# Expert weights split in half units of 1024 columns instead of whole units of 2048

## The chip, the cores and the metric

The program runs on one core of a Trainium2 chip. The metric is the device time of one execution in microseconds (us), from the start of the program to its end; lower is better. The engines are called by the profile's names: PE is the matrix engine (PEld its loading of the stationary operand), DVE the vector engine, ACT the scalar engine, POOL GpSimd, SP the queue that issues most loads.

## What is computed

Two streams (256 new frames, and 64 frames that continue a running stream, 320 tokens in all) pass two layers. A layer mixes tokens (a short convolution and a gated linear attention behind one input projection, then an output projection), adds and normalizes, and then mixes channels: dense in layer 0, experts in layer 1. The part that the change touches is the experts:

```python
def _swiglu(x, w_gate, w_up, w_down):
    return (jax.nn.silu(x @ w_gate) * (x @ w_up)) @ w_down

def _moe(x, router, w_gate, w_up, w_down):
    ...
    top_v, top_i = lax.top_k(logits, TOP_K)
    gates = jax.nn.softmax(top_v, axis=-1)
    ...
    for e in range(N_EXPERTS):
        y = y + combine[:, e:e + 1] * _swiglu(xf, w_gate[e], w_up[e], w_down[e])
```

There are 8 experts, each with three matrices of 1024 x 3584 in float32. All results are float32, and a token goes to its 2 best experts.

## The kernel before

**Split products.** A float32 product is made of three faster ones in a rounded format (fp32r). Each weight w is split into whi, which is w rounded, and wlo = w - whi; each input likewise. PE adds whi times the high input, wlo times the high input and whi times the low input. ACT makes whi by a copy that rounds (`round_unit`, L988 to L993), DVE makes wlo by a subtraction (`rest_unit`, L1247 to L1250).

**Units and rings.** Weights come in units of 1 MiB, 128 partitions x 2048 columns. SP loads them in the order of their use into `raw`, a ring of RAW = 6 units (`load`, L387 to L391); ACT and DVE write whi and wlo into rings of SPLIT = 3 units. There are 410 units: 74 for both mixers and the dense layer, and from U_MOE = 74 on 336 for the experts. Four kinds of semaphore tie a unit's way together, and each counts one per unit: `raw_landed` (a load is in), `hi_ready` (ACT is done), `lo_ready` (DVE is done; PE may start the unit, and SP may load unit n + 6 over it) and `unit_used` (PE is done; ACT may write unit n + 3 over it).

**The order of the work on experts** is written out by hand in `pair_steps`, and every engine walks the same list of steps: four pairs of experts, in each 14 chunks of 512 hidden columns (seven for one expert, seven for the other). A chunk c has two gate units, two up units and two down units; the down units are those of chunk c - 1, and one step "T" (PE transposes the hidden values, four transposes, L931) stands between the gate units. A gate or up unit is 12 matmuls (four k-tiles x three products, L901 to L903), a down unit 12 matmuls as well (two k-tiles x three products x two halves of the output, L918). A group below means these six units with their T. At the end of each pair but the last come four gather steps "X" (L877), in which PE picks the next pair's token rows. The last pair has a different end and one extra transposing step, "GT" (L936, chunk 6).

**Where the split stands in the order.** At unit n, ACT and DVE first issue the split of unit n + 2 (AHEAD = 2), and then what belongs to n:

```python
                        if not last or unit + AHEAD <= PER_PAIR:
                            rest_unit(n + AHEAD, i, PER_PAIR)
                        if part == "up" and half:
                            dve.wait_ge(unit_used, upto(n + 1, i, PER_PAIR))
                            dve.wait_ge(m_silu, upto(c + 1, i, PC))
                            dve.tensor_tensor(hm[:, c % 2, :], ...).then_inc(m_hid, 1)
```

So DVE's product `hm` (L1738), which waits until PE is through with the second up unit n, stands behind the split of n + 2 and ahead of that of n + 3. Behind `hm`, still ahead of the split of n + 3, DVE has further work in some chunks: small tables of the router in chunks 0 to 7 of the first pair (`tables`), the rows of tokens in chunks 0 to 4 of the last pair (`rows_of_tokens`), the weighted sum of finished experts in chunks 6 to 11 of the last pair (`combine`, L1723, after a gather from memory that POOL issues, L565) and `acc_lo` in chunks 11 to 13 (L1756). ACT has Silu (L1191) behind the second gate unit, the rounding of the transposed hidden values (`hT_hi`, L1215) at T, `acc_hi` (L1197) in chunks 11 to 13 of the last pair, and in chunk 13 of the last pair a load of another function table (L1193).

## Time and profile before

| what | value |
|---|---|
| median of 3 runs | 1661.7 us (1661.43 to 1662.46) |
| the profiled execution | 1663.22 us |
| its span, first to last instruction | 1661.6 us |
| PE busy | 1630.2 us, 98% of the span |
| DVE busy | 1228.0 us, 74% |
| ACT busy | 982.5 us, 59% |
| from the router's end to the last expert matmul | about 639 to 1643 us of the span |

Busy is the share of time in which at least one instruction of the engine ran. PE's matmuls overlap in the records, so a PE that is busy all the time may still have lost something: what counts for PE is the distance from one matmul's start to the next. The table is an average; the experts' stretch alone is what the change touches.

### The profile page before, as it was taken

To read this page: it belongs to the slowest core of one execution; us is meant where nothing else is said; L and a number is where in the kernel's file an instruction comes from. 1 tells how busy PE (TensorE), PEld (TensorE's weight loads), DVE (VectorE), ACT (ScalarE), POOL (GpSimd) and SP (SyncE) were. 2 spreads that over 40 slices of the span, in tenths; PEclk is the share of its full clock that TensorE was granted. 3 is DMA by queue.
4 is the path that set the end of the run, shared out by engine and by line. 5 is a ranking of instruction groups with operands and counts; after the bars stand their busy time and mean duration, and the time that the engine had idled before them with its cause. 6 is when DMAs were issued, how large, how long until landed. Compare 5 with 4: busy or idle time off the path is not lost.

```text
span 1661.6 us, 22901 instructions
## 1 busy us (share of the span) xinstructions
PE 1630.2 (98%) x8756; PEld 1413.9 (85%) x8756; DVE 1228.0 (74%) x1050; ACT 982.5 (59%) x820; POOL 82.9 (5%) x91
## 2 busy tenths in 40 slices
PE   8999999999999999999999999999999999999996
PEld 7999999999989998787888888888888888777775
DVE  4567545445454766989887888887888888989987
ACT  4453433333344536777776777776777776776663
POOL 1001111111010000000000000000000000120200
PEclk8999999999999999999999999999999999999999
DMA  9424444444444243999998999998999999999992
GB/s 297 133 97 134 152 151 146 145 145 146 150 153 153 77 134 132 354 365 362 373 376 314 363 371 364 378 363 321 369 375 368 365 364 349 354 382 377 372 352 77
DMA packets 226500, 446.58 MB, mean 269 GB/s; under 512 B 10514, under 2 KB 72640, under 8 KB 226368
## 3 DMA queue, kind: packets, MB, share of 16 engines
q1 hardware_dynamic: 223856, 434.13, 73.5%
q0 software_dynamic: 2560, 11.29, 1.8%
q8 instruction: 58, 0.95, 0.2%
q14 instruction: 26, 0.21, 0.0%
HBM read 439.87 MB, written 8.67 MB: 270 GB/s over the span
## 4 chain that ended last, share of the span: by engine, by line
PE 88%; DVE 6%; ACT 2%; issue 2%; DMA 1%; SPq 1%; DVEq 0%; ACTq 0%
PE ps L918 15%; PE ps L901 12%; PE ps L903 12%; PE ps L902 12%; PE ps L590 10%; PE ps L592 10%; PE ps L591 10%; DVE wlo L1250 2%; ACT whi L993 2%; PE ps L877 1%; PE ps L931 1%; DMA raw<-in_moe_w_up 1%; PE ps L663 1%; PE ps L622 1%; DVE xl L1285 1%
## 5 line engine op out<-in xcount | busy, mean ns | idle before, releaser
L1250 DVE TENSOR_TENSOR wlo<-raw,whi 128x2048 fp32r<-128x2048 f32 x410 | 934.5, 2291 | 255.3 <-ACT whi L993 252.6
L993 ACT ACTIVATE whi<-raw 128x2048 fp32r<-128x2048 f32 x410 | 784.5, 1915 | 244.5 <-PE ps L592 85.1
L901 PE MATMUL ps<-whi,xg 128*128 128x512 f32 x896 | 360.9, 403 | 10.5 <-DVE wlo L1250 10.2
L903 PE MATMUL ps<-whi,xg 128*128 128x512 f32 x896 | 355.1, 396 | 0.0
L902 PE MATMUL ps<-wlo,xg 128*128 128x512 f32 x896 | 354.8, 396 | 0.0
L590 PE MATMUL ps<-xh,whi 128*128 128x320 f32 x832 | 259.8, 312 | 0.3
L591 PE MATMUL ps<-xl,whi 128*128 128x320 f32 x832 | 256.9, 309 | 0.0
L592 PE MATMUL ps<-xh,wlo 128*128 128x320 f32 x832 | 256.8, 309 | 0.0
L901 PEld LDWEIGHTS ps<-whi,xg 128*128 128x128 f32 x896 | 169.3, 189 | 55.4 <-DVE wlo L1250 15.5
L903 PEld LDWEIGHTS ps<-whi,xg 128*128 128x128 f32 x896 | 169.2, 189 | 40.1
L902 PEld LDWEIGHTS ps<-wlo,xg 128*128 128x128 f32 x896 | 169.4, 189 | 36.9
L590 PEld LDWEIGHTS ps<-xh,whi 128*128 128x128 f32 x832 | 156.5, 188 | 5.2 <-DVE xl L1285 2.4
L591 PEld LDWEIGHTS ps<-xl,whi 128*128 128x128 f32 x832 | 156.5, 188 | 0.2
L592 PEld LDWEIGHTS ps<-xh,wlo 128*128 128x128 f32 x832 | 156.4, 188 | 0.0
L918 PE MATMUL ps<-whi,hT_hi 128*128 128x512 f32 x448 | 140.8, 395 | 1.3 <-DVE wlo L1250 0.7
L918 PE MATMUL ps<-whi,hT_lo 128*128 128x512 f32 x448 | 141.0, 396 | 0.0
L918 PE MATMUL ps<-wlo,hT_hi 128*128 128x512 f32 x448 | 140.5, 394 | 0.0
L918 PEld LDWEIGHTS ps<-whi,hT_hi 128*128 128x128 f32 x448 | 83.9, 188 | 21.8 <-DVE wlo L1250 2.1
L918 PEld LDWEIGHTS ps<-whi,hT_lo 128*128 128x128 f32 x448 | 84.3, 188 | 19.9
L918 PEld LDWEIGHTS ps<-wlo,hT_hi 128*128 128x128 f32 x448 | 84.2, 188 | 19.9
L1215 ACT ACTIVATE hT_hi<-ps 128x512 fp32r<-128x512 f32 x56 | 33.6, 600 | 75.1 <-PE ps L931 74.8
L590 PE MATMUL ps<-hh,whi 128*128 128x320 f32 x224 | 69.0, 308 | 0.0
(287 smaller groups left out, 1378.8 us busy)
## 6 DMA issues: line engine op xcount, KB each, us to landing
raw<-in_moe_w_gate SPq DMA_DIRECT2D x112, 1024.0 KB, 7.4
raw<-in_moe_w_up SPq DMA_DIRECT2D x112, 1024.0 KB, 7.4
raw<-in_moe_w_down SPq DMA_DIRECT2D x112, 1024.0 KB, 6.9
raw<-in_w_in SPq DMA_DIRECT2D x24, 1024.0 KB, 5.5
raw<-in_ffn_w_gate SPq DMA_DIRECT2D x14, 1024.0 KB, 5.0
raw<-in_ffn_w_up SPq DMA_DIRECT2D x14, 1024.0 KB, 5.0
raw<-in_ffn_w_down SPq DMA_DIRECT2D x14, 1024.0 KB, 5.0
raw<-in_w_out SPq DMA_DIRECT2D x8, 1024.0 KB, 5.2
```

The source lines that it names most:

```text
L590: pe.matmul(out, wh, hi, start=start and j == 0, stop=False)
L591: pe.matmul(out, wh, lo, start=False, stop=False)
L592: mm = pe.matmul(out, wl, hi, start=False, stop=stop and j == len(pairs) - 1)
L622: pe.matmul(bank[:, 0:P], mean_d[:], mean_d[:], start=True, stop=True)
L663: pe.matmul(ps[5][:, 0:T], mean_d[:], sq[:, k % 4, :], start=k == 0, stop=k == KT - 1).then_inc(var_part, 1)
L901: pe.matmul(bank[:], xh_k, wh, start=k == 0, stop=False)
L902: pe.matmul(bank[:], xh_k, wl, start=False, stop=False)
L903: mm = pe.matmul(bank[:], xl_k, wh, start=False, stop=k == KT - 1)
L918: mm = pe.matmul(ps[4 + d][:], hT[:, c % 2, k, :], slot(w, n, SPLIT, 2)[:, j, 512 * d:512 * d + 512], start=fc == 0 and k == 0 and hT is h ...
L993: act.activation(flat(whi, n, SPLIT), flat(raw, n, RAW), ACT.Copy).then_inc(hi_ready, 1)
L1215: act.activation(hT_hi[:, c % 2, :, :].rearrange("p f s -> p (f s)"), bank[:], ACT.Copy).then_inc(hT_hi_ready, 1)
L1250: dve.tensor_tensor(flat(wlo, n, SPLIT), flat(raw, n, RAW), flat(whi, n, SPLIT).bitcast(F32), ALU.subtract).then_inc(lo_ready, 1)
```

## The change

The experts' units (n >= U_MOE) are rounded, subtracted and waited for in two halves of 1024 columns. The rings keep their three and six whole units. All three semaphores now count in half units: for the other 74 units ACT, DVE and PE add 2 at once, and every wait's number is doubled. For an expert unit ACT runs two copies of 1024 columns, each with its own wait on `unit_used` and an increment of `hi_ready`; DVE runs two subtractions of 1024 columns, each with its own wait on `hi_ready` and an increment of `lo_ready`; PE waits before the unit's first and before its seventh matmul, and increments `unit_used` after its sixth and twelfth. The first half of a gate or up unit is its first two k-tiles, that of a down unit its first k-tile, which are the first six matmuls. The load of a whole unit still waits for both halves of the one that it overwrites. Silu, `hm`, the copies of finished experts and all steps' order stay.

```diff
+        def part(t, n, ring, h):
+            return flat(t, n, ring)[:, UNIT // 2 * h:UNIT // 2 * h + UNIT // 2]
+
...
                 if n >= RAW:
-                    sp.wait_ge(lo_ready, upto(n - RAW + 1, i, per))
+                    sp.wait_ge(lo_ready, upto(2 * (n - RAW + 1), i, 2 * per))
                 sp.dma_start(slot(raw, n, RAW, a), src).then_inc(raw_landed[n % RAW], 16)
...
                         bank = ps[2 * (c % 2) + (part == "up")]
-                        pe.wait_ge(lo_ready, upto(n + 1, i, PER_PAIR))
                         for j in range(4):
                             k = 4 * half + j
+                            if j % 2 == 0:
+                                pe.wait_ge(lo_ready, upto(2 * n + j // 2 + 1, i, 2 * PER_PAIR))
...
                             mm = pe.matmul(bank[:], xl_k, wh, start=False, stop=k == KT - 1)
-                        mm.then_inc(unit_used, 1)
+                            if j % 2:
+                                mm.then_inc(unit_used, 1)
...
-                        pe.wait_ge(lo_ready, upto(n + 1, i, PER_PAIR))
                         for j in range(2):
                             k = 2 * half + j
+                            pe.wait_ge(lo_ready, upto(2 * n + j + 1, i, 2 * PER_PAIR))
...
-                        mm.then_inc(unit_used, 1)
+                            mm.then_inc(unit_used, 1)
...
                 act.wait_ge(raw_landed[n % RAW], upto(16 * (n // RAW + 1), i, 16 * (per // RAW)))
-                if n >= SPLIT:
-                    act.wait_ge(unit_used, upto(n - SPLIT + 1, i, per))
-                act.activation(flat(whi, n, SPLIT), flat(raw, n, RAW), ACT.Copy).then_inc(hi_ready, 1)
+                if n < U_MOE:
+                    if n >= SPLIT:
+                        act.wait_ge(unit_used, upto(2 * (n - SPLIT + 1), i, 2 * per))
+                    act.activation(flat(whi, n, SPLIT), flat(raw, n, RAW), ACT.Copy).then_inc(hi_ready, 2)
+                    return
+                for h in range(2):
+                    act.wait_ge(unit_used, upto(2 * (n - SPLIT) + h + 1, i, 2 * per))
+                    act.activation(part(whi, n, SPLIT, h), part(raw, n, RAW, h), ACT.Copy).then_inc(hi_ready, 1)
...
-                dve.wait_ge(hi_ready, upto(n + 1, i, per))
-                dve.tensor_tensor(flat(wlo, n, SPLIT), flat(raw, n, RAW), flat(whi, n, SPLIT).bitcast(F32),
-                                  ALU.subtract).then_inc(lo_ready, 1)
+                if n < U_MOE:
+                    dve.wait_ge(hi_ready, upto(2 * (n + 1), i, 2 * per))
+                    dve.tensor_tensor(flat(wlo, n, SPLIT), flat(raw, n, RAW), flat(whi, n, SPLIT).bitcast(F32),
+                                      ALU.subtract).then_inc(lo_ready, 2)
+                    return
+                for h in range(2):
+                    dve.wait_ge(hi_ready, upto(2 * n + h + 1, i, 2 * per))
+                    dve.tensor_tensor(part(wlo, n, SPLIT, h), part(raw, n, RAW, h), part(whi, n, SPLIT, h).bitcast(F32),
+                                      ALU.subtract).then_inc(lo_ready, 1)
...
                         if part == "up" and half:
-                            dve.wait_ge(unit_used, upto(n + 1, i, PER_PAIR))
+                            dve.wait_ge(unit_used, upto(2 * (n + 1), i, 2 * PER_PAIR))
```

The waits on `unit_used` and `lo_ready` in the mixers and the dense layer are doubled in the same way and not shown.

What this does to the order is seen at two places. The first is DVE in the last pair, chunk 6: the split of unit n + 2, then `hm`, then two sums into `acc`, then the splits of n + 3, n + 4 and n + 5 (REGISTER_ALU computes the number of a wait). Before:

```order
L1249 REGISTER_ALU
L1250 TENSOR_TENSOR wlo<-raw,whi 128x2048 [waits hi_ready]
L1737 REGISTER_ALU [waits unit_used]
L1738 TENSOR_TENSOR hm<-sg,ps 128x512 [waits m_silu]
L1723 SCALAR_TENSOR_TENSOR acc<-y,gate_at,acc 128x1024 [waits y_fetched0]
L1723 SCALAR_TENSOR_TENSOR acc<-y,gate_at,acc 128x1024 [waits combined,y_fetched1]
L1249 REGISTER_ALU
L1250 TENSOR_TENSOR wlo<-raw,whi 128x2048 [waits hi_ready]
```

And in the changed kernel:

```order
L1267 TENSOR_TENSOR wlo<-raw,whi 128x1024 [waits hi_ready]
L1266 REGISTER_ALU
L1267 TENSOR_TENSOR wlo<-raw,whi 128x1024 [waits hi_ready]
L1754 REGISTER_ALU [waits unit_used]
L1755 TENSOR_TENSOR hm<-sg,ps 128x512 [waits m_silu]
L1740 SCALAR_TENSOR_TENSOR acc<-y,gate_at,acc 128x1024 [waits y_fetched0]
L1740 SCALAR_TENSOR_TENSOR acc<-y,gate_at,acc 128x1024 [waits combined,y_fetched1]
L1266 REGISTER_ALU
L1267 TENSOR_TENSOR wlo<-raw,whi 128x1024 [waits hi_ready]
```

Nothing changes its place; each subtraction has become two, with a wait of its own. The second place is PE, the gate or up unit in the last pair behind GT. Before, one wait per twelve matmuls:

```order
L901 MATMUL ps<-whi,xg 128x512 [waits lo_ready]
L902 MATMUL ps<-wlo,xg 128x512
L903 MATMUL ps<-whi,xg 128x512
L901 MATMUL ps<-whi,xg 128x512
L902 MATMUL ps<-wlo,xg 128x512
L903 MATMUL ps<-whi,xg 128x512
L901 MATMUL ps<-whi,xg 128x512
L902 MATMUL ps<-wlo,xg 128x512
```

In the changed kernel one wait per six:

```order
L906 MATMUL ps<-whi,xg 128x512 [waits lo_ready]
L907 MATMUL ps<-wlo,xg 128x512
L908 MATMUL ps<-whi,xg 128x512
L906 MATMUL ps<-whi,xg 128x512
L907 MATMUL ps<-wlo,xg 128x512
L908 MATMUL ps<-whi,xg 128x512
L903 REGISTER_ALU
L906 MATMUL ps<-whi,xg 128x512 [waits lo_ready]
L907 MATMUL ps<-wlo,xg 128x512
```

The matmuls are the same ones in the same order, and the seventh now waits as well.

## Rows read from the trace of the kernel before

**Rows 1.** The page: busy time of each engine, and the rate of loads in 40 slices.

```profile
PE 1630.2 (98%) x8756; PEld 1413.9 (85%) x8756; DVE 1228.0 (74%) x1050; ACT 982.5 (59%) x820; POOL 82.9 (5%) x91
...
GB/s 297 133 97 134 152 151 146 145 145 146 150 153 153 77 134 132 354 365 362 373 376 314 363 371 364 378 363 321 369 375 368 365 364 349 354 382 377 372 352 77
```

**Rows 2.** The page's costliest groups: count, busy us, mean ns, idle before, releaser.

```profile
L1250 DVE TENSOR_TENSOR wlo<-raw,whi 128x2048 fp32r<-128x2048 f32 x410 | 934.5, 2291 | 255.3 <-ACT whi L993 252.6
...
L901 PE MATMUL ps<-whi,xg 128*128 128x512 f32 x896 | 360.9, 403 | 10.5 <-DVE wlo L1250 10.2
```

**Rows 3.** Timeline, 1000 to 1012 us, second pair: start, duration, engine, line, operation.

```profile
1001.59 0.63 PE L918 MATMUL ps<-whi,hT_hi 128*128 128x512 f32 x2
...
1001.79 1.92 ACT L993 ACTIVATE whi<-raw 128x2048 fp32r<-128x2048 f32 x1 [0.88 <-PE ps L903]
...
1003.75 2.29 DVE L1250 TENSOR_TENSOR wlo<-raw,whi 128x2048 fp32r<-128x2048 f32 x1
...
1007.19 0.40 PE L901 MATMUL ps<-whi,xg 128*128 128x512 f32 x1
```

**Rows 4.** Timeline of ACT: the rounding of the transposed hidden values, once per group.

```profile
657.36 0.60 ACT L1215 ACTIVATE hT_hi<-ps 128x512 fp32r<-128x512 f32 x1 [1.24 <-PE ps L931]
...
796.91 0.60 ACT L1215 ACTIVATE hT_hi<-ps 128x512 fp32r<-128x512 f32 x1 [1.25 <-PE ps L931]
...
1189.82 0.60 ACT L1215 ACTIVATE hT_hi<-ps 128x512 fp32r<-128x512 f32 x1 [1.31 <-PE ps L931]
1206.98 0.60 ACT L1215 ACTIVATE hT_hi<-ps 128x512 fp32r<-128x512 f32 x1 [1.31 <-PE ps L931]
...
1402.93 0.60 ACT L1215 ACTIVATE hT_hi<-ps 128x512 fp32r<-128x512 f32 x1 [1.32 <-PE ps L931]
...
1621.21 0.60 ACT L1215 ACTIVATE hT_hi<-ps 128x512 fp32r<-128x512 f32 x1 [1.47 <-PE ps L931]
```

**Rows 5.** Timeline, last pair, chunk 6: DVE, then PE in a narrower window.

```profile
1501.32 0.68 DVE L1738 TENSOR_TENSOR hm<-sg,ps 128x512 f32<-128x512 f32 x1
1501.91 2.67 DVE L1723 SCALAR_TENSOR_TENSOR acc<-y,gate_at,acc 128x1024 f32<-128x1024 f32 x2
1504.50 6.69 DVE L1250 TENSOR_TENSOR wlo<-raw,whi 128x2048 fp32r<-128x2048 f32 x3
...
1506.84 0.50 PE L901 MATMUL ps<-whi,xg 128*128 128x512 f32 x1 [1.32 <-DVE wlo L1250]
1507.18 0.39 PE L902 MATMUL ps<-wlo,xg 128*128 128x512 f32 x1
```

**Rows 6.** Timeline, last pair, chunk 11: operations of 1024 columns on ACT and DVE.

```profile
1590.00 1.04 ACT L1197 ACTIVATE acc_hi<-acc 128x1024 fp32r<-128x1024 f32 x1
...
1595.32 1.21 DVE L1756 TENSOR_TENSOR acc_lo<-acc,acc_hi 128x1024 fp32r<-128x1024 f32 x1
1596.46 6.68 DVE L1250 TENSOR_TENSOR wlo<-raw,whi 128x2048 fp32r<-128x2048 f32 x3
```

**Rows 7.** Timeline, 625 to 650 us, the first expert unit that is split behind the router.

```profile
642.43 3.70 ACT L993 ACTIVATE whi<-raw 128x2048 fp32r<-128x2048 f32 x2
...
644.37 6.70 DVE L1250 TENSOR_TENSOR wlo<-raw,whi 128x2048 fp32r<-128x2048 f32 x3 [4.21 <-ACT whi L993]
...
646.72 0.50 PE L901 MATMUL ps<-whi,xg 128*128 128x512 f32 x1 [2.33 <-DVE wlo L1250]
```

**Rows 8.** Windows: length, busy us (x count) of PE, PEld, DVE, ACT, POOL; PEclk, DMA, GB/s.

```profile
647.70:651.00 3.30, 3.30 (x9) 2.55 (x9) 3.30 (x2) 0.71 (x1) 0.00 (x0) 0.50 1.02 309
...
1500.00:1600.00 100.00, 93.71 (x409) 74.52 (x408) 90.88 (x54) 69.97 (x46) 10.46 (x4) 1.00 1.01 374
```

**Rows 9.** Timeline of PE, last pair, chunk 13: two late starts.

```profile
1630.29 0.73 PE L918 MATMUL ps<-whi,hT_hi 128*128 128x512 f32 x2 [0.74 <-DVE wlo L1250]
...
1637.11 0.73 PE L918 MATMUL ps<-whi,hT_hi 128*128 128x512 f32 x2 [0.54 <-DVE hT_lo L1764]
```

**Rows 10.** The chain of waits, 1380 to 1500 us: the longest piece (start, us, what).

```profile
1456.41 15.37 DMA raw<-in_moe_w_up
```

More of the change, by code:

```diff
@@ L604, in two_tiles @@
                         if j == KT - 1:
-                            mm.then_inc(unit_used if half else tile_done, 1)
+                            mm.then_inc(unit_used, 2) if half else mm.then_inc(tile_done, 1)
             def x_hi(k):
@@ L756, in mixer @@
                 hooks = {1: gates, 5: turn_kv, 6: scores, 7: states, 8: outputs, 9: mean_squares}
-                pe.wait_ge(lo_ready, U_IN[l] + 1)
+                pe.wait_ge(lo_ready, 2 * (U_IN[l] + 1))
                 two_tiles(U_IN[l], lambda j: pe.wait_ge(xl_ready, KT * 2 * l + j + 1))
@@ L769, in mixer @@
                     n = U_IN[l] + u
-                    pe.wait_ge(lo_ready, n + 1)
+                    pe.wait_ge(lo_ready, 2 * (n + 1))
                     for half in range(2):
@@ L774, in mixer @@
                         mm = split_product(ps[(2 * u + half) % 4][:, 0:T], by_tile(n, KT, half), True, True)
-                        mm.then_inc(unit_used if half else tile_done, 1)
+                        mm.then_inc(unit_used, 2) if half else mm.then_inc(tile_done, 1)
                     if u in hooks:
@@ L780, in mixer @@
                     n = U_OUT[l] + u
-                    pe.wait_ge(lo_ready, n + 1)
+                    pe.wait_ge(lo_ready, 2 * (n + 1))
                     if u == 0:
@@ L789, in mixer @@
                         mm = split_product(ps[m % 4][:, 0:T], by_tile(n, KT, half, y_hi, y_lo), True, True)
-                        mm.then_inc(unit_used if half else tile_done, 1)
+                        mm.then_inc(unit_used, 2) if half else mm.then_inc(tile_done, 1)
                 pe.wait_ge(rows_ready[l], 1)
@@ L800, in dense_mixer @@
                         n, q = U_FFN + j, j // 2
-                        pe.wait_ge(lo_ready, upto(n + 1, c, PER_CHUNK))
+                        pe.wait_ge(lo_ready, upto(2 * (n + 1), c, 2 * PER_CHUNK))
                         if j == 0:
@@ L812, in dense_mixer @@
                             mm = split_product(ps[bank][:, 0:T], by_tile(n, KT, half), True, True)
-                            mm.then_inc(unit_used if half else tile_done, 1)
+                            mm.then_inc(unit_used, 2) if half else mm.then_inc(tile_done, 1)
                     n = U_FFN + 4
-                    pe.wait_ge(lo_ready, upto(n + 1, c, PER_CHUNK))
+                    pe.wait_ge(lo_ready, upto(2 * (n + 1), c, 2 * PER_CHUNK))
                     pe.wait_ge(d_added, upto(4, c, 8))
@@ L822, in dense_mixer @@
                             mm = split_product(ps[4 + m][:, 0:T], [(wh, wl, hh[:, k, :], hl[:, k, :])], k == 0, k == 3)
-                    mm.then_inc(unit_used, 1)
+                    mm.then_inc(unit_used, 2)
                     n = U_FFN + 5
-                    pe.wait_ge(lo_ready, upto(n + 1, c, PER_CHUNK))
+                    pe.wait_ge(lo_ready, upto(2 * (n + 1), c, 2 * PER_CHUNK))
                     for m in range(4):
@@ L830, in dense_mixer @@
                                  for k in range(4)]
-                        split_product(ps[m][:, 0:T], pairs, True, True).then_inc(unit_used if m == 3 else tile_done, 1)
+                        mm = split_product(ps[m][:, 0:T], pairs, True, True)
+                        mm.then_inc(unit_used, 2) if m == 3 else mm.then_inc(tile_done, 1)
                 pe.wait_ge(d_added, 8 * FC + 4)
@@ L921, in pair @@
                                                        stop=fc == FC - 1 and k == 3 and hT is hT_lo)
-                        mm.then_inc(unit_used, 1)
+                            mm.then_inc(unit_used, 1)
                     else:
@@ L1110, in mixer @@
                         if half:
-                            act.wait_ge(unit_used, n + 1)
+                            act.wait_ge(unit_used, 2 * (n + 1))
                         else:
@@ L1137, in dense_mixer @@
                                 if half:
-                                    act.wait_ge(unit_used, upto(U_FFN + j + 1, c, PER_CHUNK))
+                                    act.wait_ge(unit_used, upto(2 * (U_FFN + j + 1), c, 2 * PER_CHUNK))
                                 else:
@@ L1188, in pair @@
                         if part == "gate" and half:
-                            act.wait_ge(unit_used, upto(n + 1, i, PER_PAIR))
+                            act.wait_ge(unit_used, upto(2 * (n + 1), i, 2 * PER_PAIR))
                             act.wait_ge(m_hid, upto(max(0, c - 1) + 1, i, PC))
@@ L1199, in pair @@
                             a = c // FC
-                            act.wait_ge(unit_used, upto(n + 1, i, PER_PAIR))
+                            act.wait_ge(unit_used, upto(2 * (n + 1), i, 2 * PER_PAIR))
                             if last and a:
@@ L1480, in mixer @@
                         if half:
-                            dve.wait_ge(unit_used, n + 1)
+                            dve.wait_ge(unit_used, 2 * (n + 1))
                         else:
@@ L1506, in dense_mixer @@
                                 if half:
-                                    dve.wait_ge(unit_used, upto(n + 1, c, PER_CHUNK))
+                                    dve.wait_ge(unit_used, upto(2 * (n + 1), c, 2 * PER_CHUNK))
                                 else:
@@ L1518, in dense_mixer @@
                                 if j == 4 or m == 3:
-                                    dve.wait_ge(unit_used, upto(n + 1, c, PER_CHUNK))
+                                    dve.wait_ge(unit_used, upto(2 * (n + 1), c, 2 * PER_CHUNK))
                                 else:
@@ L1532, in clear @@
             def clear():
-                dve.wait_ge(unit_used, U_OUT[1] + UNITS_OUT)
+                dve.wait_ge(unit_used, 2 * (U_OUT[1] + UNITS_OUT))
                 dve.memset(xt_hi[TOK[2]:P, 2, :].bitcast(F32), 0.0)
```

## The prediction

> **What bounds the kernel now.** I read the page first. PE is busy for 98% of the span, DVE for 74%, ACT for 59% [rows 1]; so PE sets the time, and a change on DVE and ACT can only pay where PE waits for them. The page's groups name such waits: before L901, PE's idle time is ended by DVE's wlo, 10.2 us in all [rows 2]. That figure is too low, because a matmul is recorded with 0.39 us [rows 5] while the next one starts after 0.23 (2.79 us for the twelve of a unit, below): 0.16 is missing from each idle time. I therefore measured the loss by distances between starts.
>
> The timeline of the second pair shows the undisturbed rhythm [rows 3]. From PE's start on a unit at 1001.59 to its start two units later at 1007.19 are 5.60 us, so 2.80 us a unit (2.79 in the third pair, whose groups are 6 x 0.01 shorter). When PE starts unit n (1001.59), ACT gets the slot that unit n - 1 has left 0.20 us later, rounds n + 2 in 1.92, DVE subtracts in 2.29 until 1006.04, and PE needs the result at 1007.19. The way through the ring takes 4.45 us of 5.60, and 1.15 are spare: PE is the bound there. In the third pair a whole group of six units with its T takes 1206.98 - 1189.82 = 17.16 us [rows 4]; the same distance in the other two stretches shows the loss. In the first pair, 657.36 to 796.91 are 8 groups in 139.55 us, 2.3 over 8 x 17.16. In the last, 1402.93 to 1621.21 are 12 groups in 218.28, 12.4 over 12 x 17.16, of which I give 0.6 to the GT step (three transposes, by the four of a T: a group of 17.16 less six units of 2.79 is 0.42), so 11.8.
>
> Why PE waits there is seen in chunk 6 of the last pair [rows 5]. DVE's hm waits for PE's second up unit n, but it stands behind the split of n + 2, which through the ring ends 4.45 us after PE began n, that is 1.65 after PE has finished it. Only then come hm (0.59 to the next start), the extra work E, and the split of n + 3, which PE wants 5.58 us after the end of n. This leaves for E 5.58 - 1.57 - 0.59 - 2.29 - 0.06 = 1.07 us (1.57 since DVE starts the next operation 0.08 before the record of the last ends; 0.06 is from DVE's end to PE's start). E here is 1504.50 - 1501.91 = 2.59, so PE should be 1.5 late; its row at 1506.84 shows 1.32 idle beside the overlap. The tables and sums of the other chunks are the same case with another E.
>
> **The change, part by part.**
> 1. *Cost on DVE.* 336 subtractions of 2048 become 672 of 1024. Back to back, the three at 1504.50 give (6.69 - 2.29)/2 = 2.20 us apart [rows 5]; an operation of 1024 with two inputs takes 1.21, and the next starts 1.14 after it [rows 6]. So a unit costs 2.28 instead of 2.20: 0.08, or 27 us more over 336 units. Beside PE, DVE then needs 12 x 1.14 + 2 x 0.60 = 14.9 us of 17.16 in a group, so it is covered; in a group with E = 2.59 it is 17.5, 0.3 over, once in each of three groups, which the spare time gained below takes up.
> 2. *Cost on ACT.* A rounding of 1024 takes 1.04 [rows 6] and one of 2048 takes 1.92 [rows 3]: at most 0.16 more a unit, 54 us in all, on an engine with 679 us idle. Covered by PE.
> 3. *Cost on PE.* 336 more waits, one before each seventh matmul. Between units PE already has such a wait, satisfied ahead of time, and the group of 17.16 contains six of them at 2.79 a unit; twelve starts at the usual 0.23 are the same 2.79. Lower bound 0. The upper bound is a wait that really holds: the restart at 1506.84 has 0.34 to the next start instead of 0.23 [rows 5], so 0.11 each, 37 us in all. I take 0, since the nearest row is a satisfied wait. Loads, POOL and SP's queue keep their number and order; SP's wait is met earlier, never later.
> 4. *Gain inside the ring.* ACT may round the first half of n + 2 when PE is half through n - 1, at -1.40 + 0.20 = -1.20 counted from PE's start of n, and is done at -0.16; DVE has the first half at +1.09. The second half starts on ACT at +0.20 and is through DVE at 0.20 + 1.04 + 0.04 + 1.21 = +2.49, instead of +4.45. That is before PE ends n at 2.80, so hm no longer stands behind it. Then 0.20 + 0.59 + E + 1.21 + 0.06 must fit into 5.58: E up to 3.52 instead of 1.07. The 2.59 of chunks 6 to 8 fits. In chunk 11 the two sums and acc_lo come to about 2.59 + 1.14 = 3.7, just over the edge, so 0.2 stay there. What is late next is nothing of this chain, so I count the whole of both stretches, less that: 2.3 + 11.6.
> 5. *Gain at the start.* Behind the router, ACT comes to unit 2 of the experts only at 642.43, its copy of it begins there, and PE, which could go on at 644.2 (2.33 of idle time and the missing 0.16 back from there), starts at 646.72 [rows 7]. In halves: 642.43 + 1.04 + 0.04 + 1.21 + 0.06 = 644.8, so the wait of 2.5 shrinks to 0.6, 1.9 gained. Just behind that wait the granted clock is 0.50 for 3.3 us, half of what 2.4 GHz is, and PE starts 9 matmuls where it would start 14 [rows 8], 1.65 us lost. The window with the waits of 1.5 us in chunks 6 to 8 has a mean granted clock of 1.00 [rows 8], so behind a wait of 0.6 I expect no such stretch: 1.65 gained. Together 3.6.
> 6. *Gain at the end.* In chunk 13 PE starts late twice, by 0.74 and 0.54 of idle time, with the missing 0.16 by 0.9 and 0.7 [rows 9]: the first behind ACT's table load, the second behind DVE's order. Both chains are shortened by over 1 us; 1.6 gained.
> 7. *Not gained.* Chunks 4 and 5 of the last pair waited for a load that took 15.37 us [rows 10], while POOL's gathers used the same engines. A late load now leads to PE 1.04 + 1.21 + 0.1 = 2.4 after it lands instead of 4.3, which helps, but PE no longer gives the loads time by waiting elsewhere. I keep back 1.0.
>
> Sum: 2.3 + 11.6 + 3.6 + 1.6 - 1.0 = 18.1 us less. From the profiled execution's 1663.2 this is 1645.1; the median of the runs stands 1.5 below that execution, so 1643.6.
>
> **A rule against it.** In rows 5 three held subtractions follow each other 2.20 apart though each is recorded with 2.29. The Trainium skill, VectorE: DVE Perf Modes, The DRAIN you can't avoid, says that the next operation doesn't start until the pipe is empty, and its rules for authors say to minimize the number of operations. By that rule the halves would cost more than in part 1, and the sum would be that of the first rival below; the rows don't bear it out for this form.
>
> **The rivals.**
> - *Each half pays in full.* If no half overlaps its neighbour and each waits 0.04 for its semaphore, a half costs 1.25, a group 12 x 1.25 + 2 x 0.72 = 16.4. Quiet groups stay hidden. Groups with E = 2.59 need 19.0 and run 1.9 over, less the 2 us of spare time once: about 3.5 us of their 4.7 stay. The same in chunk 11 (2 us) and the first pair (1) leaves 12 of 18.1: about 1650. For it: the new halves wait on ACT's halves one by one. Against: rows 5 and 6.
> - *Loads become the bound.* A unit is 1.049 MB; at the highest rate of any slice, 382 GB/s [rows 1], it takes 2.74 us, and PE wants one in 17.16/6 = 2.86. The reserve is 4%. After the delay of [rows 10] the loads would catch up by only 0.12 a unit, so in chunks 4 to 8 the waits would move from DVE to the loads. Of 6 us there 4 stay: 1647. Against: the load isn't asked for later than before.
> - *The seventh matmul's wait costs PE time* (slower). It decides from 18.1/336 = 0.054 us a wait. At the 0.11 of a real restart [rows 5] it is 37 us, so 19 slower: 1680. For it: the wait is in the middle of an accumulation, where the trace of before has none. Against: satisfied waits between units show nothing.
> - *No change*: the first halves would have to reach PE no earlier, as when ACT, in order, is held by the second half's wait ahead of Silu or hT_hi, and these come late for PE in turn. ACT's 41% of idle time speaks against it; 1661.
>
> **How the numbers follow.** Forecast 0.64, first rival 0.14, loads 0.12, slower 0.06, no change 0.04. The predicted time is the forecast's, 1643.6. Its own bounds are 1640.5 (the 1.0 kept back, the 0.2 of chunk 11 and the 0.6 of the start gained as well, and 1.3 for some 20 groups of the second pair's kind, 0.07 longer than the third pair's, that might run like these) and 1647; reaching to the loads and the first rival gives 1640.5 to 1650.5, which leaves out the last two and the tails. A measurement can tell 0.2% (3.3 us) from no change: faster 0.90, same 0.04, slower 0.06.
>
> **What would show it.** Groups in both stretches near 17.2 us; hm right behind PE's second up unit instead of behind wlo; subtractions of about 1.21 us, starting 1.14 apart when back to back; no low clock behind the router's end; PE's unit at 2.79 with no gap at its seventh matmul. I would be wrong if that gap shows, if groups with sums stay near 18.8, or if ACT's idle time is ended by loads for many units.

## The result, and the profile after

| what | before | changed |
|---|---|---|
| median, six runs each | 1661.72 us (1660.17 to 1662.46) | 1649.24 us (1648.18 to 1653.08) |
| ratio, 95% interval | | 0.9929, 0.9916 to 0.9942 |
| profiled execution, its span | 1663.22, 1661.6 us | 1648.18, 1646.5 us |
| PE, DVE, ACT busy | 1630.2, 1228.0, 982.5 us | 1621.7, 1244.0, 1015.9 us |

The change is 12.5 us faster by the medians, 0.71%. 1643.6 had been forecast, with a range of 1640.5 to 1650.5. So the sign and the range held, and a third of the gain of 18.1 is missing. The two profiled executions stand 15.1 us apart in their spans: the one of before lay 1.5 above its median, the one of the change 1.1 below. Where the steps are compared below, it is against these 15.1. A unit has the number of its place in its pair, from 0 to 83; chunk c begins at unit 6c. A quiet group is one in which PE waits for nothing.

First the costliest groups of the page, changed kernel, as in [rows 2]:

```profile
L1267 DVE TENSOR_TENSOR wlo<-raw,whi 128x1024 fp32r<-128x1024 f32 x672 | 778.2, 1219 | 54.2 <-ACT whi L1004 53.0
L1004 ACT ACTIVATE whi<-raw 128x1024 fp32r<-128x1024 f32 x672 | 676.7, 1054 | 94.1 <-PE ps L924 55.1
L906 PE MATMUL ps<-whi,xg 128*128 128x512 f32 x896 | 358.8, 400 | 2.8 <-DVE wlo L1267 2.6
```

There are 672 halves on either engine, of 1.22 and 1.05 us each, and PE's idle time ended by wlo has gone from 10.2 to 2.6 us. The change's DVE is busy for 16 us more, ACT for 33. Next ACT's timeline at the lines that answer to [rows 4]:

```profile
653.41 0.60 ACT L1226 ACTIVATE hT_hi<-ps 128x512 fp32r<-128x512 f32 x1 [1.61 <-PE ps L937]
790.74 0.60 ACT L1226 ACTIVATE hT_hi<-ps 128x512 fp32r<-128x512 f32 x1 [2.17 <-PE ps L937]
...
1124.24 0.60 ACT L1226 ACTIVATE hT_hi<-ps 128x512 fp32r<-128x512 f32 x1
...
1150.47 0.60 ACT L1226 ACTIVATE hT_hi<-ps 128x512 fp32r<-128x512 f32 x1 [1.54 <-PE ps L937]
1167.64 0.60 ACT L1226 ACTIVATE hT_hi<-ps 128x512 fp32r<-128x512 f32 x1 [2.17 <-PE ps L937]
...
1397.81 0.60 ACT L1226 ACTIVATE hT_hi<-ps 128x512 fp32r<-128x512 f32 x1 [2.18 <-PE ps L937]
...
1606.73 0.60 ACT L1226 ACTIVATE hT_hi<-ps 128x512 fp32r<-128x512 f32 x1 [2.18 <-PE ps L937]
```

The eight groups of the first stretch take 137.33 us, 17.17 each: no loss is left there. The twelve groups of the last stretch take 208.92 instead of 218.28; 12 x 17.16 + 0.6 would be 206.5, so 2.4 are left. A place that the prediction didn't look at has become longer: from 1124.24, in the last chunk of the second pair, to 1150.47 in the first of the third are 26.23 us, where before it was 23.90. Sorted by stretches, the 15.1 us are: start 3.95 (from 657.36 to 653.41), first stretch 2.22, last stretch 9.36, end 0.62, quiet groups of the middle pairs 1.3, and -2.33 at the border of the second and third pair.

Of the 3.95, 0.69 are there before PE starts the first expert unit (638.64 before, 637.95 after).

**Start.** Timelines of ACT, DVE and PE behind the router, changed kernel, as in [rows 7]:

```profile
641.75 3.89 ACT L1004 ACTIVATE whi<-raw 128x1024 fp32r<-128x1024 f32 x4
...
642.83 8.04 DVE L1267 TENSOR_TENSOR wlo<-raw,whi 128x1024 fp32r<-128x1024 f32 x7 [3.35 <-ACT whi L1004]
...
644.11 0.50 PE L906 MATMUL ps<-whi,xg 128*128 128x512 f32 x1 [0.41 <-DVE wlo L1267]
```

ACT begins at 641.75, the first half has gone through DVE 2.3 us later, and PE stands idle for 0.41 instead of 2.33. No stretch of granted clock 0.50 follows: the trace records none from here until PE has finished at 1636.7.

**Sums of the last pair.** DVE's timeline, chunk 6, changed kernel, as in [rows 5]:

```profile
1489.89 4.68 DVE L1267 TENSOR_TENSOR wlo<-raw,whi 128x1024 fp32r<-128x1024 f32 x4
1494.48 0.68 DVE L1755 TENSOR_TENSOR hm<-sg,ps 128x512 f32<-128x512 f32 x1
1495.08 2.67 DVE L1740 SCALAR_TENSOR_TENSOR acc<-y,gate_at,acc 128x1024 f32<-128x1024 f32 x2
1497.66 4.62 DVE L1267 TENSOR_TENSOR wlo<-raw,whi 128x1024 fp32r<-128x1024 f32 x4
```

The same E of 2.58 now leads from 1497.66 to a first half at 1498.88 and to PE's start at 1498.93, 0.3 late instead of 1.5. The split of n + 2 still stands ahead of hm as four halves back to back, ending 4.68 us after 1489.89; what has changed is that behind the sums PE waits for one half instead of a whole.

**The new stop.** Timelines of ACT, then PE, where the loop over the middle pairs jumps back (changed kernel):

```profile
1133.75 1.09 ACT L1219 ACTIVATE ys<-ps 128x512 f32<-128x512 f32 x2 [1.27 <-PE ps L924]
1138.87 3.90 ACT L1004 ACTIVATE whi<-raw 128x1024 fp32r<-128x1024 f32 x4 [4.03 <-PE ps L908]
...
1141.23 0.50 PE L906 MATMUL ps<-whi,xg 128*128 128x512 f32 x1 [1.77 <-DVE wlo L1267]
```

and the same place on ACT before:

```profile
1141.09 1.09 ACT L1208 ACTIVATE ys<-ps 128x512 f32<-128x512 f32 x2 [0.95 <-PE ps L918]
1142.06 3.72 ACT L993 ACTIVATE whi<-raw 128x2048 fp32r<-128x2048 f32 x2
```

Before, ACT goes on in the same moment. In the changed kernel it stands for 4 us though the slot has long been free. DVE stands for 4.2 us at a jump back of its own, and PE is 1.9 late. What differs is the length of the code: from one jump back to the next, which is one pair of experts, the trace has 271 instructions on ACT and 222 on DVE before, and 424 and 390 after (waits, jumps and register computations counted as well). Each second half brings an operation and, for nearly all, the register computation of its wait's number (84 and 84 more on DVE). In the DMA view of this place (changed kernel, 1134 to 1148 us) stands a queue that loads instructions:

```profile
q14 instruction: 4, 0.03, 0.6%
```

In the same window of the kernel before, q14 isn't there at all. In the whole execution it has 26 packets before and 43 after, of 8 KB each.

### The profile page after: what moved, and what is told of

It is laid out like the page before. It is cut to its first block, busy times and chain, and to the rows that moved or that the text cites. A ratio compares the mean times of both kernels' runs of the same rounds, so it can differ in the third digit from the quotient of the medians.

```text
span 1646.5 us, 24383 instructions
## 1 busy us (share of the span) xinstructions
PE 1621.7 (98%) x8756; PEld 1412.2 (86%) x8756; DVE 1244.0 (76%) x1386; ACT 1015.9 (62%) x1156; POOL 92.0 (6%) x91
## 4 chain that ended last, share of the span: by engine, by line
PE 92%; DVE 4%; issue 1%; DMA 1%; ACT 1%; SPq 1%; DVEq 0%; ACTq 0%
PE ps L924 18%; PE ps L906 12%; PE ps L908 12%; PE ps L907 12%; PE ps L593 11%; PE ps L595 10%; PE ps L594 10%; PE ps L881 1%; PE ps L937 1%; DMA raw<-in_moe_w_up 1%; PE ps L666 1%; DVE wlo L1267 1%; PE ps L625 1%; PE ps L767 1%; DVE xl L1302 0%
## 5 line engine op out<-in xcount | busy, mean ns | idle before, releaser
L1267 DVE TENSOR_TENSOR wlo<-raw,whi 128x1024 fp32r<-128x1024 f32 x672 | 778.2, 1219 | 54.2 <-ACT whi L1004 53.0
L1004 ACT ACTIVATE whi<-raw 128x1024 fp32r<-128x1024 f32 x672 | 676.7, 1054 | 94.1 <-PE ps L924 55.1
L1262 DVE TENSOR_TENSOR wlo<-raw,whi 128x2048 fp32r<-128x2048 f32 x74 | 169.6, 2292 | 133.5 <-ACT whi L1000 133.5
L1000 ACT ACTIVATE whi<-raw 128x2048 fp32r<-128x2048 f32 x74 | 141.2, 1908 | 78.3 <-PE ps L595 75.3
```

The costliest lines, as they stand in the source:

```text
L1000: act.activation(flat(whi, n, SPLIT), flat(raw, n, RAW), ACT.Copy).then_inc(hi_ready, 2)
L1004: act.activation(part(whi, n, SPLIT, h), part(raw, n, RAW, h), ACT.Copy).then_inc(hi_ready, 1)
L1262: dve.tensor_tensor(flat(wlo, n, SPLIT), flat(raw, n, RAW), flat(whi, n, SPLIT).bitcast(F32), ALU.subtract).then_inc(lo_ready, 2)
L1267: dve.tensor_tensor(part(wlo, n, SPLIT, h), part(raw, n, RAW, h), part(whi, n, SPLIT, h).bitcast(F32), ALU.subtract).then_inc(lo_ready, 1)
```

## Experiments

Ratios are to the kernel before, run on the same chip beside each. e0 to e3 shared one set of runs of it (median 1661.94), e4 to e7 one (1662.27), e8 to e11 one (1662.22). The chip isn't the same one for all three sets, so runs of different sets are best compared by their ratios. The theories: **A**, the stop at the jump back comes from a loop body too long to be kept, and costs about 2 us here; **B**, the half release of a slot by PE (what the prediction's part 4 begins with) is worth little; **C**, the early hand-over of the first half from DVE to PE is worth most of the gain.

**e0_change_again.** The changed kernel, once more.

> The change itself again, beside the others of this call. If its scatter (1648.2 to 1653.1) is its own, it shows again: 1648 to 1653, median near 1649.2. If it came from the first set of runs alone, it narrows to within 1 us as the kernel before does.

Measured: 1648.13 us, ratio 0.9919 (0.9906 to 0.9933). The stop is there again, with 3.37 us of idle time on ACT ahead of the row at 1139.45; PE is 1.3 late.

**e1_loop_whole.** Whole units in the looped pairs, halves in the first and last pair.

```diff
-                if n < U_MOE:
+                if n < U_MOE or looped(i):
```

(the same for PE's waits and for both splits)

> The change with whole units in the two looped pairs, where the kernel before had no late units. Theory A (the longer loop bodies of ACT and DVE stop both engines for about 4 us at the loop's jump back): the stop of 3.85 us on ACT between the second and the third pair is gone, the distance of hT_hi over that boundary falls from 26.2 to 23.9 us, and the time is about 2.3 us under the change's, near 1647. Rival (the stop is by chance, or from the store of finished rows at that place): it stays or comes and goes, and the time is the change's within 1 us.

Measured: 1652.77 us, 0.9945 (0.9931 to 0.9958): slower than the change, a miss. The body came down to 340 instructions on ACT and 306 on DVE only, because a whole unit here waits in an instruction of its own (84 more of them on DVE than in the kernel before, 69 on ACT). ACT's timeline shows two idle times of about 4 us:

```profile
1134.47 1.09 ACT L1233 ACTIVATE ys<-ps 128x512 f32<-128x512 f32 x2 [0.91 <-PE ps L936]
1139.82 3.71 ACT L1014 ACTIVATE whi<-raw 128x2048 fp32r<-128x2048 f32 x2 [4.27 <-issue]
...
1149.65 1.92 ACT L1014 ACTIVATE whi<-raw 128x2048 fp32r<-128x2048 f32 x1 [3.83 <-PE ps L916]
```

Only the first is a stop at the jump back. The second is ended by PE: PE starts its next unit 4.4 us late, and needs 5.2 us for the one after it, at half its clock (last section). The third pair took 254.2 us instead of the 249.6 of the change. So halves cushion a stop, and on ACT the length that decides lies below 340. DVE, with 306, has no stop of its own: its next instruction runs 0.30 us behind the jump, and two q14 packets stand at this place instead of the change's four.

**e2_before_longer_loop.** The kernel before, with waits that are met long ago in the looped pairs, four per unit on ACT and on DVE (bodies 439 and 390).

```diff
+                if in_loop:
+                    for old in (x_ready, xl_ready, centered, squared):
+                        act.wait_ge(old, 1)
```

> The kernel before, with four waits that are long met behind each rounding and each subtraction of the looped pairs, so that ACT's loop body has 439 instructions (271 before, 424 in the change) and DVE's 390 (222 and 390). Theory A: ACT and DVE stop for about 4 us at the jump back, and PE loses some 2 us there, so 1663.5 to 1664.5. Rival (only the halves bring the stop): no stop, 1661.7 within 1 us.

Measured: 1668.77 us, 1.0043 (1.0028 to 1.0059). Both idle times appear on ACT (3.99 and 3.82 us, the second again ended by PE), with four q14 packets in the same 20 us, and the third pair takes 254.3 instead of 247.4. A holds: without any halves, more instructions in the body make the stop.

**e3_release_whole.** The change, with PE returning both halves of a slot at the unit's end.

```diff
-                            if j % 2:
-                                mm.then_inc(unit_used, 1)
+                        mm.then_inc(unit_used, 2)
```

> The change, but PE gives a unit's ring slot back at the unit's end alone. By the prediction's own working (part 4) the half release carries 1.4 us of the spare time: DVE's hm starts 0.8 us behind PE's second up unit instead of right behind it, room for extra work falls from 3.5 to 2.1 us, chunks 6 to 8 of the last pair lose 0.5 each and chunk 11 1.5 or more: about 1652.5. Theory B (ACT stands in order behind Silu, and DVE then has four halves back to back, so that the ring's early release isn't what ends last): hm's place and the time stay within 1 us of the change's.

Measured: 1648.89 us, 0.992 (0.9907 to 0.9934), within 0.8 of e0. B holds: the earlier release is worth less than a measurement tells. The starts of the units say the same: no unit outside the jump back is more than 0.12 longer than in e0.

**e4_handover_whole.** The change, with PE waiting for both halves at the unit's first matmul.

```diff
-                            if j % 2 == 0:
-                                pe.wait_ge(lo_ready, upto(2 * n + j // 2 + 1, i, 2 * PER_PAIR))
+                            if j == 0:
+                                pe.wait_ge(lo_ready, upto(2 * n + 2, i, 2 * PER_PAIR))
```

> The change, but PE waits for both halves before a unit's first matmul. Theory C (the early start of PE on a first half carries a good part of the gain): the room for extra work falls by one subtraction, 1.14 us, so chunks 6 to 8 of the last pair lose about 0.8 each, chunk 11 and the start 1.1 each with a stretch at the lower clock behind one or both (1.6 each), the pair boundary and the late load 1.1 each: 1654 to 1657. Rival (nearly all comes from the overlap of ACT's and DVE's halves): within 2 us of the change's.

Measured: 1656.17 us, 0.9962 (0.9947 to 0.9976), 8.0 us above e0 and 7.1 by the ratios. The loss is clear, but more than half of it doesn't speak for C. Its profiled execution is 8.8 us longer than that of the change, and the starts of the units tell where:

| where | before to change | before to e4 |
|---|---|---|
| first six expert units | 3.3 shorter | 2.3 shorter |
| the eight groups behind them | 2.2 shorter | 1.7 shorter |
| last pair | 10.1 shorter | 7.6 shorter |
| jump back | 2.3 longer | 5.1 longer |

At the places where the change gains 15.6, e4 still gains 11.6, and the hand-over is worth about the other 4.0: 0.9 at the start and 0.3, 0.7, 0.7 and 1.1 in chunks 6, 7, 8 and 11. The rest is 0.5 of the pace of quiet groups (last section), less 0.3 for loads that were late in the change only. Another 2.8 are lost at the jump back, where the kernel before has no stop (1.3 of them because PE's clock falls to 0.50 for 3.4 us there), and 2.0 ahead of the first unit and in other quiet groups. So C holds for a quarter of the gain, not for most of it.

**e5_unrolled.** The change, with the second pair written out ahead of the loop, whose body then runs once, so that nothing jumps back.

```diff
+            pair(1, PAIR)
-            with act.Fori(1, pairs) as i:
+            with act.Fori(2, pairs) as i:
```

(the same for PE and DVE)

> The change with the second pair written out on PE, ACT and DVE ahead of the loop, which then runs its body once with these inputs and jumps back never. Theory A: the stop of ACT and DVE between second and third pair is gone, the third pair takes about 247.5 us like the second instead of 249.0 to 249.6, and the time falls by 1.5 to 2.3 us, to 1646 to 1646.7. If the stop weren't the jump's, the third pair stays at 249 or more and the time stays.

Measured: 1646.11 us, 0.9903 (0.9887 to 0.9919). ACT's timeline has no stop:

```profile
1134.88 1.09 ACT L1220 ACTIVATE ys<-ps 128x512 f32<-128x512 f32 x2 [1.20 <-PE ps L924]
1135.90 3.91 ACT L1005 ACTIVATE whi<-raw 128x1024 fp32r<-128x1024 f32 x4
```

From the window of the DMA view in which the change has four q14 packets one is left, and the unit that was 1.9 late is on time. The third pair takes 247.33 us instead of 249.59, or 248.98 in e0. By the ratios alone this gain isn't clear: the intervals of e5 and e0 overlap.

**e6_unrolled_table_late.** e5, with ACT's table load moved from the second up unit's step behind the first half of the last down units.

```diff
-                            if last and c == PC - 1:
-                                act.preload_act_table_set(LOG_EXP)
+                        if last and part == "down" and c == PC - 1 and not half:
+                            act.preload_act_table_set(LOG_EXP)
```

> The same with ACT's function table loaded behind its last rounding instead of ahead of three of them. Theory D (the end's late start before the last down units stands behind the table load of 1.3 us, which delays ACT, DVE, hm and so hT_lo): the late start of 0.5 us idle before the last down units goes, and with the small one before it 1.0 us: 1645 to 1645.7. Rival (hT_lo is late only for its place behind a subtraction): no change against the unrolled one.

Measured: 1646.85 us, 0.9903 (0.9887 to 0.9919), not to be told from e5. The trace shows the gain at its place all the same: two of the last down units are 0.24 and 0.79 us shorter. What hides it are the quiet groups of this execution, in sum 0.84 longer in the first and in the third pair each, where the code is e5's (see the last section), and another 1.1 in chunks 4 to 8 of the last pair, where e5 waited less for loads.

**e7_unrolled_table_gathers_apart.** e6, and POOL's second gather waits until DVE has both rows of tokens, so that the two gathers don't run together in the transfer engines.

```diff
+            pool.wait_ge(rows_known, 2)
```

> The same again, and POOL starts its second three gathers a chunk later. Theory E (the late loads of chunks 4 and 5 of the last pair come from the six gathers at once): ACT's waits for loads in the last pair, 2 to 3 us of which PE feels about 1.3, fall by half or more: 0.5 to 1.3 us less. Rival (the same bytes cost the loads the same time, wherever they are): no change, or a wait for the gathered rows in chunk 6 that costs more.

Measured: 1645.45 us, 0.9895 (0.9879 to 0.991), the best version. In the last pair, units 30, 31 and 39 were 0.22, 0.11 and 0.28 long in the change, and are not here. But they aren't in e0, e3 and e5 either, where the gathers run as in the change, so this isn't the edit's doing. Against e5 and e6 the medians differ by 0.7 and 1.4, less than the interval. Whether gathers apart gain anything stays open.

**e8_before_unrolled.** e5's edit on the kernel before (the written-out pair stands behind the reading of the loop's count instead of ahead of it).

> The kernel before with its second pair written out, so that its loop's body runs once and there is no jump back; nothing else differs. Theory A (the stop comes of a loop body that ACT or DVE must fetch again at the jump back): the kernel before has no stop there (ACT body 271 instructions, DVE 222), so writing out gives nothing: ratio to before 0.999 to 1.001, third pair 247.3 to 248.3 us, no idle time of ACT over 3 us at that place. If instead every jump back costs some time, or the written out code runs better by itself, it is 1 to 3 us faster than before, and the 2 us of the same edit on the change would not be the stop's.

Measured: 1662.25 us, 0.9999 (0.9991 to 1.0008). Written-out code gains nothing by itself, so what e5 gained was the stop's.

**e9_before_act_longer**, **e10_before_dve_longer**, **e11_before_act_a_little.** e2's waits on one engine alone: four per unit on ACT (body 439), four on DVE (390), one on ACT (312).

> The kernel before; only ACT's loop body is made longer, by four waits per unit that are met long ago (439 instructions instead of 271); DVE's body stays at 222. Theory A with each engine fetching for itself: ACT stops 3 to 4 us at the jump back, once or twice, DVE has no stop of its own, and the kernel is 4 to 7 us slower than before. If the stop needs both engines' code on the one queue: less than half of that.

> The kernel before; only DVE's loop body is made longer, by four waits per unit that are met long ago (390 instructions instead of 222); ACT's body stays at 271. Theory A with each engine fetching for itself: DVE stops 2.5 to 4 us at the jump back while ACT runs on; PE then waits for wlo by about as much: 2 to 5 us slower than before. If only ACT's stop counts: no difference to before.

> The kernel before; ACT's loop body has one met wait per unit more, 312 instructions instead of 271; DVE's stays at 222. If the body of 340 of the whole-unit loop stopped since it lies on three code pages of 256 instructions where 271 lies on two, 312 may do so as well: ACT stops 3 to 4 us once, 2 to 5 us slower. If the limit is between 312 and 340, or 271 already is at it: no stop, no difference to before. I hold it for even.

| run | ACT, DVE body | median, us | ratio, 95% interval |
|---|---|---|---|
| e9 | 439, 222 | 1668.44 | 1.0036 (1.0023 to 1.005) |
| e10 | 271, 390 | 1662.97 | 1.0007 (0.9998 to 1.0015) |
| e11 | 312, 222 | 1668.42 | 1.0034 (1.0021 to 1.0047) |

ACT alone makes the whole 6 us, and 312 instructions do as much as 439: here it is a step, between 271 and 312, not a price per instruction. Each of the three has two q14 packets at this place, where e2, with both bodies longer, has four. e11's timeline, ACT and then PE:

```profile
1144.63 3.71 ACT L995 ACTIVATE whi<-raw 128x2048 fp32r<-128x2048 f32 x2 [4.11 <-issue]
...
1154.44 1.92 ACT L995 ACTIVATE whi<-raw 128x2048 fp32r<-128x2048 f32 x1 [3.82 <-PE ps L905]
...
1148.92 0.79 PE L903 MATMUL ps<-whi,xg 128*128 128x512 f32 x1 [4.02 <-DVE wlo L1257]
```

In e10 DVE has a stop of its own while ACT runs on. DVE's timeline, then PE's:

```profile
1142.99 6.70 DVE L1257 TENSOR_TENSOR wlo<-raw,whi 128x2048 fp32r<-128x2048 f32 x3 [2.49 <-ACT whi L995]
...
1145.34 0.50 PE L903 MATMUL ps<-whi,xg 128*128 128x512 f32 x1 [0.75 <-DVE wlo L1257]
```

ACT's whi for this subtraction began at 1140.10 and took 1.9, so DVE could have started at 1142.0 and is 1.0 late; PE loses 0.9. The cause is the same (DVE's next instruction runs 4.35 us behind its jump), but most of this stop lies beside ACT's work, and the median doesn't show it. The 2 to 5 us expected were too much.

## Why the prediction was right or wrong

1. *DVE's and ACT's costs (parts 1 and 2)* were right in size and in being covered. DVE's busy time grew by 16 us where 27 was worked out from starts (records of neighbours overlap, so busy time counts less); quiet groups of the first stretch take 17.17 as expected.
2. *PE's wait (part 3)* costs nothing: units between T steps take 2.79 to 2.80 us, with no gap at the seventh matmul. The rival on the slower side is refuted.
3. *The ring (part 4)* gave 2.22 of 2.3 and 9.36 of 11.6, but not in the way described. The prediction let ACT round the first half early, because PE returns half a slot, and counted room for E of 3.52. e3 takes that release away and loses nothing measurable. The step that failed is "that is before PE ends n at 2.80, so hm no longer stands behind it". ACT is in order: Silu, which waits for PE's second gate unit, stands ahead of the halves, and they then come back to back. DVE's timeline of chunk 11, changed kernel, has it:

```profile
1576.02 4.63 DVE L1267 TENSOR_TENSOR wlo<-raw,whi 128x1024 fp32r<-128x1024 f32 x4 [0.50 <-ACT whi L1004]
1580.57 0.68 DVE L1755 TENSOR_TENSOR hm<-sg,ps 128x512 f32<-128x512 f32 x1
1581.17 2.46 DVE L1740 SCALAR_TENSOR_TENSOR acc<-y,gate_at,acc 128x1024 f32<-128x1024 f32 x2
1583.56 1.21 DVE L1773 TENSOR_TENSOR acc_lo<-acc,acc_hi 128x1024 fp32r<-128x1024 f32 x1
1584.70 3.48 DVE L1267 TENSOR_TENSOR wlo<-raw,whi 128x1024 fp32r<-128x1024 f32 x3
```

   PE ended unit n at 1579.75, hm starts 0.8 later, behind the four halves, and E is 3.53. PE's next unit starts at 1585.96, 0.64 late; so the room is about 2.9 and not 3.52. It grew by some 1.8 from 1.07. The hand-over to PE is 1.1 of it, the time between a half and a whole behind E, and hm's place, on which the prediction built, is nearly 0.8: DVE starts on a half that ACT rounded in 1.05, not on a unit that took 1.92. By e4 the hand-over to PE is worth about 4.0 of the 15.6 us gained at the start, in the first stretch and in the last pair. That the other 11.6 come from the hand-over between ACT and DVE is left over by elimination, with e3 and e4; no run takes it away alone.

   Not all of the 11.8 that the prediction counted in the last pair was this chain. 1.1 were lost at units 28 and 29, where loads came late, and 1.6 behind PE's restart in chunk 11, where the clock was at 0.50 (window before, columns as in [rows 8]):

```profile
1599.90:1603.30 3.40, 3.40 (x10) 2.52 (x9) 3.24 (x2) 0.00 (x0) 0.00 (x0) 0.51 0.94 318
```

   The change has no such stretch there. And of the 2.2 that are missing against 11.6, up to 1.1 are this execution's own: the last pair of e0, the same kernel, is 1.1 shorter, mostly in chunks 5 to 8.
4. *Start (part 5)*: 3.95 against 3.6. Both terms came as told, 1.92 for 1.9 in the wait and 1.54 for 1.65 in the clock, and a wait of 0.41 was followed by no low clock, as [rows 8] had let expect. That this lands on 3.95 is partly luck, as 0.69 lie ahead of the first unit. The clock's term belongs to the profiled execution and not to the kernel: e10, whose code is that of before at this place, has the same wait of PE and a full clock behind it, with 16 matmuls where before had 9:

```profile
647.37 0.50 PE L903 MATMUL ps<-whi,xg 128*128 128x512 f32 x1 [2.34 <-DVE wlo L1257]
...
648.00:651.30 3.30, 3.30 (x16) 2.69 (x15) 3.30 (x2) 1.84 (x2) 0.00 (x0) 1.00 0.78 289
```

   Of the six profiled executions with the code of before, four have the low clock at the start and three the one in chunk 11. The profiled one of before has both, some 3.1 us. That may be why it stands above its median, and why the medians show less gain than the profiles.
5. *End (part 6)*: 0.62 of 1.6. The first late start is gone (0.9). The second is not; PE's timeline in chunk 13:

```profile
1621.98 0.73 PE L924 MATMUL ps<-whi,hT_hi 128*128 128x512 f32 x2 [0.63 <-DVE hT_lo L1781]
```

   and DVE's:

```profile
1612.61 4.63 DVE L1267 TENSOR_TENSOR wlo<-raw,whi 128x1024 fp32r<-128x1024 f32 x4 [1.94 <-ACT whi L1004]
...
1618.89 2.36 DVE L1267 TENSOR_TENSOR wlo<-raw,whi 128x1024 fp32r<-128x1024 f32 x2
1621.16 0.69 DVE L1781 TENSOR_TENSOR hT_lo<-ps,hT_hi 128x512 fp32r<-128x512 f32 x1
```

   The words "both chains are shortened by over 1 us" failed: hT_lo stands behind both halves, and where an operation waits for a whole unit, two halves are longer than one unit (2.36 against 2.29). The chain begins at ACT's table load, as e6 shows.
6. *Loads (part 7)*: 1.0 kept back. In chunks 4 to 6 of the last pair ACT's waits are ended by loads, by 0.22 to 2.70 us each, and PE loses about 0.3 in units 30 and 31 and 0.3 in chunk 6. In e0, the same kernel, it loses none of this. So the rival of the loads had the place right, and its price of 3.4 too high: 0.6 in one execution and nothing in another. ACT's timeline:

```profile
1463.03 2.01 ACT L1004 ACTIVATE whi<-raw 128x1024 fp32r<-128x1024 f32 x2 [2.70 <-DMA raw<-in_moe_w_gate]
1465.74 2.01 ACT L1004 ACTIVATE whi<-raw 128x1024 fp32r<-128x1024 f32 x2 [0.70 <-DMA raw<-in_moe_w_up]
```

7. *What was missing*: the stop at the jump back, 2.3 us in the profiled change and 1.7 in e0. The prediction costed the new instructions by their execution alone and took the register computations that the changed order shows as nothing. The Trainium skill, Runtime: NRT & Kernel Launch, Instruction fetch mechanics, states that a taken branch whose target lies outside the two pages held forces a fetch before the engine goes on. That speaks against this change and should have been a term of the sum. The traces agree: the stop comes with the taken branch, with packets of the instruction queue beside it, and goes without the branch (e2, e5, e11). The page gives no length of a loop's body that is safe: with its pages of 256 instructions, where a body lies counts too. Here ACT stopped with 312 and DVE didn't with 306.
8. *Each half pays in full*, the first rival: halves back to back start 1.14 apart and are recorded with 1.22, so the rule of the Trainium skill, VectorE: DVE Perf Modes, The DRAIN you can't avoid (the next operation begins when the pipe is empty) isn't borne out for this form either. The same section adds that an operation which isn't held starts earlier, which the prediction left out; the 0.08 of overlap fits that. That rival's time, 1650, lies nearest to the result all the same. That is by chance: its halves overlap here all the same, and the stop that it doesn't know makes the difference.

So 18.1 less 2.3 (stop), 2.2 (last stretch) and 1.0 (end), and 2.5 more for the quiet groups, the start and the loads kept back, gives the 15.1 of the profiled executions; the medians have 12.5, as one of these executions lay above and one below its median.

## What to carry to other kernels

Handing a unit over in halves pays where the consumer waits for one unit behind some other work, and at each of the two hand-overs: here 0.8 us between ACT and DVE and 1.1 between DVE and PE, each time such a wait is on PE's path. Splitting the return of the slot buys nothing while the producer is held by something else in its order. Before more instructions go into a loop's body, count the body per engine and look for the instruction queue at the jump back: here ACT stood for 4 us as soon as its body went from 271 to 312 instructions, and writing one round out ahead of the loop removed the stop. What a stop costs the bound engine depends on what the ring holds: with halves PE was 1.3 to 2.0 late, with whole units 4.0 to 4.4, and there its clock fell too, which cost 1.7 to 2.5 more. And before a term is taken from one profile, look whether other executions of the same code have it.

## What was not expected of the hardware

- The stop at a jump back, above: 3.4 to 4.3 us on ACT, a step in the body's length and not a slope. ACT went on with 271 and stopped with 312; DVE went on with 306 (e1) and stopped with 390. Which length holds exactly, and how it depends on where the body lies in memory, wasn't tried.
- Quiet stretches run at two paces. A group of six units takes either 17.17 or 17.23 us, and keeps to it over a whole pair: 17.17 in the second pair of the profiled change, 17.23 in that of e0, which is the same kernel; 17.17 in the third pair of e5, 17.23 in that of e6, where the code is the same. Before had 17.23 in the second pair and 17.17 in the third. The pace was seen to change at a pair's border or behind a wait of PE, at a granted clock of 1.00 throughout. A pair is 0.84 us longer at the slower one, four pairs 3.4. What sets it stays open. For edits worth 1 us the distances between PE's starts tell more than the medians.
- A stop of PE can bring its clock down as well. The windows of e11 and of the change behind the stop (length, then busy us and counts of PE, PEld, DVE, ACT, POOL, and the granted clock):

```profile
1147.50:1154.30 6.80, 5.38 (x13) 4.21 (x14) 5.77 (x3) 3.12 (x3) 0.00 (x0) 0.50 0.66 220
```

```profile
1141.30:1148.00 6.70, 6.70 (x29) 5.43 (x30) 6.70 (x7) 6.70 (x9) 0.00 (x0) 1.00 0.66 249
```

  In e11 the clock is at 0.50, the lower level of 1.2 GHz, behind 4.02 us of idle PE, and PE starts 13 matmuls; behind the change's 1.77 it stays at 1.00, with 29. In e11 the unit behind the stop takes 5.28 us, 2.5 more than its 2.79, and in e9, where the low clock lasts 3.4 us instead of 6.8, 4.46. So up to 2.5 of the distance between 6 us with whole units and 2 with halves are this, and it is also what ACT's second idle time of 3 to 4 us waits for. The same stop of PE isn't always followed by a low clock, as e10 shows at the start (above).
